# The split of three gate weights, the window stores and the Exp table load moved in a one-core decoder layer

## What is computed

```python
def decoder_layer(x, ple, attend, ...):
    x = x + 0.5 * swiglu(rms_norm(x, g_ffn1), w1_ffn1, w3_ffn1, w2_ffn1)
    z = rms_norm(x, g_mix) @ w_in + b_in
    q, k, v, u, vg = jnp.split(z, SPLITS, axis=-1)
    attn_out, k_state, v_state = attend(q, k, v)
    vg = layer_norm(jax.nn.gelu(vg), gm_ln_g, gm_ln_b)
    gm_out = jax.nn.gelu(u) * chunk_spatial_mix(vg, gm_w_s, gm_b_s)
    x = x + jnp.concatenate([attn_out, gm_out], axis=-1) @ w_out + b_out
    x = x + 0.5 * swiglu(rms_norm(x, g_ffn2), w1_ffn2, w3_ffn2, w2_ffn2)
    gate = jax.nn.sigmoid(rms_norm(x, g_ple) @ w_ple_gate)
    x = x + gate * (ple @ w_ple_proj)
    return x, k_state, v_state, vg
```

## Time and profile before

| | us |
|---|---|
| median of 3 runs (lowest, highest) | 942.73 (941.79, 942.81) |
| the profiled execution, own time | 941.79 |
| its span in the trace | 940.0 |
| PE busy | 927.0 |
| VectorE busy | 744.5 |
| ScalarE busy | 587.7 |
| GpSimd busy | 236.2 |

### The profile page before, as it was taken

How to read it: one execution, slowest core, us unless ns; L and a number is a source line. 1 busy time by engine, 2 the same in 40 slices (tenths; PEclk the granted TensorE clock), 3 DMA queues, 4 the chain that set the end, 5 groups by cost and what they waited for, 6 DMA issues and landing times.

```text
span 940.0 us, 19778 instructions
## 1 busy us (share of the span) xinstructions
PE 927.0 (99%) x7702; PEld 915.9 (97%) x7702; DVE 744.5 (79%) x1290; ACT 587.7 (63%) x976; POOL 236.2 (25%) x184
## 2 busy tenths in 40 slices
PE   7999999999999999999999999999999999999997
PEld 7999999999999999989999999999999999999897
DVE  6979977888888786567866588988788988869586
ACT  7748746666667575756544566766676676657343
POOL 0212222223222221100319412223222322222221
PEclk9999999999999999999999999999999999999999
DMA  8958888778887779531133798877777887778802
GB/s 249 179 102 169 151 172 159 142 142 161 169 158 144 134 163 244 103 81 46 52 96 91 139 176 161 170 152 152 164 149 131 176 173 142 155 165 170 146 24 92
DMA packets 256506, 134.99 MB, mean 144 GB/s; under 512 B 15643, under 2 KB 252533, under 8 KB 256397
## 3 DMA queue, kind: packets, MB, share of 16 engines
q1 hardware_dynamic: 177820, 93.55, 36.1%
q0 software_dynamic: 78256, 39.33, 33.8%
q10 hardware_dynamic: 336, 0.84, 0.2%
HBM read 131.15 MB, written 3.59 MB: 143 GB/s over the span
## 4 chain that ended last, share of the span: by engine, by line
PE 55%; issue 27%; POOL 9%; DMA 3%; DVE 3%; ACT 1%; SPq 1%; POOLq 0%; DVEq 0%; ACTq 0%
PE ps L2079 30%; PE ps L1990 19%; POOL w_lo L1264 4%; POOL w_lo L1272 4%; PE ps L2421 2%; PE ps L2024 1%; PE ps L2108 1%; DMA w_lo<-in_w_ffn_dram 1%; DMA w_lo<-in_w_ple_gate_dram 1%; DMA x_rows<-in_x_prompt_dram 1%; PE ps L2297 1%; POOL w_lo L1236 1%; PE ps L2326 1%; DMA w_raw<-in_w_ffn_dram 1%; DVE w_lo L1686 0%
## 5 line engine op out<-in xcount | busy, mean ns | idle before, releaser
L2079 PE MATMUL ps<-xo_hi,w_lo 128*128 128x260 f32 x1008 | 284.8, 283 | 0.0
L2079 PE MATMUL ps<-xo_hi,w_hi 128*128 128x260 f32 x1008 | 284.4, 282 | 0.0
L2079 PE MATMUL ps<-xo_lo,w_hi 128*128 128x260 f32 x864 | 244.3, 283 | 0.0
L2079 PEld LDWEIGHTS ps<-xo_hi,w_hi 128*128 128x128 f32 x1008 | 189.9, 188 | 0.0
L2079 PEld LDWEIGHTS ps<-xo_hi,w_lo 128*128 128x128 f32 x1008 | 189.9, 188 | 0.0
L1500 DVE TENSOR_TENSOR w_lo<-w_raw,w_hi 128x512 fp32r<-128x512 f32 (+1 forms) x180 | 174.7, 984 | 15.1 <-ACT w_hi L941 7.4
L2079 PEld LDWEIGHTS ps<-xo_lo,w_hi 128*128 128x128 f32 x864 | 162.7, 188 | 0.0
L2079 PE MATMUL ps<-hop_hi,w_hi 128*128 128x260 f32 x560 | 158.6, 283 | 0.1
L2079 PE MATMUL ps<-hop_hi,w_lo 128*128 128x260 f32 x560 | 158.4, 283 | 0.0
L2079 PE MATMUL ps<-hop_lo,w_hi 128*128 128x260 f32 x560 | 158.2, 282 | 0.0
L1264 POOL DMA_DIRECT2D w_lo<-in_w_ffn_dram x60 | 76.8, 1279 | 276.1 <-ACT w_lo L948 276.1
(11 more groups left out here) (320 smaller groups left out, 2066.2 us busy)
## 6 DMA issues: line engine op xcount, KB each, us to landing
w_raw<-in_w_ffn_dram SPq DMA_DIRECT2D x88, 256.0 KB, 4.5
w_lo<-in_w_ffn_dram POOLq DMA_DIRECT2D x88, 256.0 KB, 5.3
w_a<-in_w_ffn_dram SPq DMA_DIRECT2D x36, 512.0 KB, 5.9
w_raw<-in_w_ffn_dram SPq DMA_DIRECT2D x20, 512.0 KB, 6.1
w_a<-in_w_ffn_dram SPq DMA_DIRECT2D x32, 192.0 KB, 4.0
w_raw<-in_w_ffn_dram SPq DMA_DIRECT2D x32, 192.0 KB, 4.2
w_lo<-in_w_ffn_dram POOLq DMA_DIRECT2D x32, 192.0 KB, 5.2
w_raw<-in_w_in_dram SPq DMA_DIRECT2D x10, 512.0 KB, 4.6
```

Source lines behind the costliest of these rows:

```text
L2079: ins = pe.matmul(ps[:, b, 0:Q], w[:, cc, k * P:(k + 1) * P], m_, start=(first and k == 0 and t == 0), stop=(k == kn - 1 and t == 2), skip ...
```

## The change

1. Tail: gates 1, 2 and 3 leave `summed`. ScalarE makes only their rounded parts, three in a row after the second FFN, and GpSimd subtracts, three tensor_tensor in place of three DMAs.
2. The splits `("hi", "next", 3)` and `("hi", "next", 4)` leave the end of the FFN list; with the looser condition on `gemm` (0 in place of 2), the splits of `in` 3 and `in` 4 are now placed at `gemm` (1, 2) and (2, 2), on ScalarE and on GpSimd. VectorE's rest of `in` 4 moves from (1, 7) to (2, 7), that of `in` 13 from (11, 7) to (12, 0).
3. `stat_spread` and `evac` 0 and 1 move from (2, 1) to (2, 0).
4. The five `norm` steps move from (11, 7) to (12, 0), behind `evac` 11.
5. The four window stores are issued by ScalarE, after its copies, not by SyncE.
6. The 64x1 Exp goes; the table load then stands before the first Exp of the attention.

```diff
-                steps += [("lo", "next", 2), ("hi", "next", 3), ("hi", "next", 4)]
+                steps.append(("lo", "next", 2))
...
-        (2, 1): [("stat_spread",), ("evac", 0), ("evac", 1)],
+        (2, 0): [("stat_spread",), ("evac", 0), ("evac", 1)],
...
-        (11, 7): [("s_take",), ("norm_rsqrt",), ("norm", 3), ("norm", 4), ("norm", 0), ("norm", 1), ("norm", 2)],
+        (11, 7): [("s_take",), ("norm_rsqrt",)],
+        (12, 0): [("norm", 3), ("norm", 4), ("norm", 0), ("norm", 1), ("norm", 2)],
...
-        summed += [("up", 1, n) for n in range(3, N_STD)] + last_keys(1)[:2] + last_keys(1)[3:6]
+        summed += [("up", 1, n) for n in range(3, N_STD)] + last_keys(1)[:2]
...
-        low_steps = [("gemm", 1, 7), ("gemm", 4, 7)] + [("gemm", u - 2, 7) for u in range(8, N_IN)] + [("gemm", 12, 7), ("gemm", 13, 2), ("out", 0, 4)]
+        low_steps = [("gemm", 2, 7), ("gemm", 4, 7)] + [("gemm", u - 2, 7) for u in range(8, N_IN - 1)] + [("gemm", 12, 0), ("gemm", 12, 7), ("gemm", 13, 2), ("out", 0, 4)]
...
-                elif u == 8:
-                    store_windows()
...
-                if kind == "gemm" and arg[1] == (2 if arg[0] < 6 else 5) and 2 < arg[0] < 13:
+                if kind == "gemm" and arg[1] == (2 if arg[0] < 6 else 5) and 0 < arg[0] < 13:
...
-                elif kind == "scores" and arg[0] == 0:
-                    nc.scalar.activation(s_st[:, 6:7], ones[0:64, 0:1], ACT.Exp)
...
+                    act.wait_ge(kv_taken, 4)
+                    act.dma_start(o["v_win_prompt"][0, 0].rearrange("w h d -> w (h d)"), v_rows[:, NB - 1, :]
+                                  ).then_inc(out_done, 16)
+                    act.dma_start(o["k_win_prompt"][0, 0].rearrange("w h d -> w (h d)"), k_rows[:, 0, :]
+                                  ).then_inc(out_done, 16)
...
-            split_hi(last_keys(1)[5])
+            for key in last_keys(1)[3:6]:
+                split_hi(key)
...
-            split_lo(last_keys(1)[5])
+            for key in last_keys(1)[3:6]:
+                split_lo(key)
```

More of the change, by code:

```diff
@@ L781, in _ @@
             load_ffn(0, 2)
[L783 to L793, removed]
             def load_mixer():
@@ L1117, in _ @@
                     nc.scalar.activation(k_rows[0:TS, 1, :], ps[0:TS, 7, 2 * P:3 * P], ACT.Copy).then_inc(kv_taken, 1)
+                    act.wait_ge(kv_taken, 4)
[3 more added lines that the diff above has]
+                                  ).then_inc(out_done, 16)
+                    act.dma_start(o["v_win_sample"][0, :, W - 1].rearrange("b h d -> b (h d)"), v_rows[0:TS, NB, :]
+                                  ).then_inc(out_done, 16)
+                    act.dma_start(o["k_win_sample"][0, :, W - 1].rearrange("b h d -> b (h d)"), k_rows[0:TS, 1, :]
+                                  ).then_inc(out_done, 16)
                 elif kind == "soft":
```

## The result

| | before | changed |
|---|---|---|
| median of 4 runs, us (lowest, highest) | 942.77 (941.79, 943.33) | 949.90 (948.41, 950.10) |
| the profiled execution, own time | 941.79 | 950.45 |
| its span in the trace | 940.0 | 948.7 |

The ratio of the runs is 1.0074, with a 95% interval of 1.0056 to 1.0091: 7.1 us slower, where 1.0 faster was forecast. In the trace the last matmul starts at 942.81, before at 934.17: 8.6 us later.

A forecast was written before the change was run, and what follows sets the result against it. PE was taken to bound the kernel, busy 927.0 of 940.0 us. Terms -2.9 + 0 + 1.6 + 0.2 = -1.1 took 941.79 to 940.7; the median, 0.94 above, was forecast at 941.7 us, range 939.3 to 945.0.

The forecast's parts named there:

- `in` 3: Start of `in` 3: its correction DMA, issued later, still lands before PE wants it; cost 0, bounds 0 and 4.4 us.
- I take 6.7: Correction DMA of `in` 3: issue to landing taken as 6.7 us, from another DMA, landing 1.0 before it is wanted.
- its bound of 12.1: Correction DMA of `in` 3: worst landing time of the rows, 12.1 us, which would stall PE 4.4 us.
- The rival: At `in` 3: correction DMA meets window copies and a load, takes 9.0 to 12.1 us; 943.0 to 947.7, chance 0.15.
- Tail: Gate 1 and sixth proj group: 4.0 us gained, 1.1 lost as GpSimd's subtraction holds VectorE's add; net -2.9 us.
- the 4.0: Gate 1 in the tail: 2.40 us of gap plus 1.58 of lower clock behind it, all to be regained.
- `kv_turn`: Ahead of the first softmax transpose: ScalarE's four issues and table load stall PE, +1.6 us, bounds 1.1 and 2.7.
- no double price of the load: Between ScalarE's copies and first Exp: a rival had the table load cost twice, 943.0 us, chance 0.05.
- the slack: Ahead of the first softmax transpose: PE had 0.8 us to spare, subtracted from ScalarE's 2.3 us delay.
- Norms: First use of the five norms, now behind `evac` 11: a stall of 0.3, taken as +0.2 us, bounds -0.3 and +1.5.
- the mechanism named there: At the norms: GpSimd's later product of the norms may hold one VectorE operation for its length, giving the +1.5 bound.
- Part 3: `stat_spread` a k-step earlier: finds its root just made, 0 to -0.1 us, taken as 0.

The follow-up runs named there:

- after_in3_back: Changed kernel with the correction DMA of `in` 3 issued at its old place again, ahead of the clearing and the mask: 943.43 us, ratio 1.0020.
- kv_only: Kernel before with only the four window stores issued by ScalarE and the small Exp removed: 944.51 us, ratio 1.0019.
- after_copies_late: Changed kernel with SyncE's two window copies issued behind the load of `in` 7: 943.82 us, ratio 1.0030.
- stores_act: Kernel before with only the four window stores issued by ScalarE, the small Exp kept: 945.96 us, ratio 1.0040.
- after_copies_in13: Changed kernel with the window copies behind the load of `in` 7 and VectorE's rest of `in` 13 back ahead of `evac` 11: 943.32 us, ratio 1.0021.
- no_preload: Kernel before with only the small Exp removed, the window stores left on SyncE: 941.13 us, ratio 0.9995.

## Why the prediction was wrong

- **`in` 3: wrong, and it decided the result.** The step that failed is "I take 6.7, since the loads queued ahead at 362.0 are done by 366, though SyncE's window copies follow at 367". The place of the issue was right (365.97 for 366.07), the landing was 13.4 for 6.7, outside its bound of 12.1 as well. The number of the other DMA was taken without what was queued behind it; the copies cost 6.3 us of landing (13.4 against 7.1). The rival had the mechanism and the lower clock, at a chance of 0.15, and its 946.1 is still under the 949.9: it put the worst at 4.4 + 1.6, the trace shows 5.4 + 2.4. It was said to decide from 7.7 us to landing on; that a DMA may take 9.0 with only loads ahead was in the rows, and should have moved the likeliest case itself.
- **Tail: right in mechanism, off in size.** The wait is gone, the clock behind it too, the add took 2.52 (2.3 to 2.5 forecast), the gap was 1.11 more (1.1). The term that was mis-sized is the 4.0: 1.58 of it is a lower clock that comes in some executions only.
- **`kv_turn`: right, in part by luck.** The issues 1.6 (1.6), the load 1.28, the stall 1.7 (1.6), no double price of the load, and no lower clock behind the gap of 2.0. What it didn't see is that the slack depends on when `in` 5 lands. In the changed kernel PE came 7.8 us late, and ScalarE stood ready and waited for it (3.30 us, above). Without that the stall was 1.9 in after_in3_back and 2.1 in kv_only.
- **Norms: the bound was right, the central value wrong.** 0.3 at the first use as worked out. With the +1.2 behind it makes 1.5, the very edge of the bound. The +1.2 did not come by the mechanism named there; it came from the rest of `in` 13, which stood in the diff and which the prediction didn't cost.
- **Part 3**: no effect, as forecast.
- The recorded sum has a slip that changes nothing: 941.79 - 1.1 + 0.94 is 941.6, not 941.7.
- The range, 939.3 to 945.0, was made of terms each bounded by a row of one execution; the changed kernel lies 5 us above it.

## What to carry to other kernels

In these traces the same DMA landed after anything from 7.1 to 15.9 us, and from 7.1 to 13.4 the difference was made by two copies queued just behind it. Before moving one, list what every queue issues in the 10 us behind its new place, and give it the time of a row that had the same neighbours. A step moved off an idle stretch cost its length here (1.2 us, the rest of `in` 13), though its engine was far from busy. And where a subtraction given to GpSimd starts just ahead of a two-input operation of VectorE (2.52 us in place of 0.69), one wait that lets the short one go first gives the time back: with it, part 1 gave the fastest kernel of all these runs.

## What was not expected of the hardware

- The same DMA of 512 KB, at the same place, landed after 9.0 to 10.0 us in seven traces of kernels with the old order and the copies behind it, and after 15.9 in an eighth. In that one the copies are 16 packets of 65,024 bytes, each 2.4 to 3.3 us long.
- The length of a gap of PE doesn't decide on the clock behind it: at the softmax, gaps of 2.43 us (kv_only), 2.67 (after_copies_late) and even 3.51 (stores_act) left the granted clock at 1.00, and one of 2.65 (after_copies_in13) was followed by 3.4 us at the lower level; in the tail, gaps of 2.4 to 2.6 had either behind them. The windows of stores_act, its gap and what follows, columns as in the earlier trace rows:

```profile
385.40:388.70 3.30, 0.17 (x3) 0.00 (x1) 0.88 (x5) 2.94 (x11) 0.00 (x0) 1.00 1.24 234
388.70:392.20 3.50, 3.50 (x30) 3.50 (x30) 3.17 (x14) 2.71 (x6) 0.00 (x0) 1.00 0.10 29
```

- An issue of a DMA on ScalarE took 0.28 to 0.61 us in all these traces, but 0.94 in one (after_copies_late), 0.96 in one (after_copies_in13) and 1.34 in one (stores_act); each time it was the second of the four window stores. Why is open.
- Of the table load no trace shows more than its 1.28 us: copies end, 0.02 us, load, 0.01 us, Exp. The Trainium skill (ScalarE: Activation LUTs, "What ACT_TABLE_LOAD costs") gives about 1283 ns for the load and about 1380 ns of drain; no_preload, where the load stood between two busy stretches, shows the load and no drain.
